# Two layers written out in one block of engine programs instead of a loop of blocks

## The chip, the core and the metric

One core of one Trainium2 chip. The metric is the device time of one execution in microseconds (us), the median of three. The engines are TensorE (PE; its weight loads are shown as PEld), VectorE (DVE), ScalarE (ACT), GpSimd (POOL) and SyncE (SP), which here issues the DMAs.

## What is computed

A token stream of 512 x 1024 floats passes through two layers (DEPTH = 2) and then a second block of another kind. All data are float32, and each layer is

```python
mod = c_act @ ada_w[l] + ada_b[l]
sh1, sc1, g1, sh2, sc2, g2, sh3, sc3, g3 = jnp.split(mod, N_MOD, axis=-1)
h = modulate(rms_norm(x, norm_ffn1[l]), sh1, sc1)
x = x + 0.5 * g1[:, None, :] * swiglu(h, ffn1_w_in[l], ffn1_w_out[l])
h = modulate(rms_norm(x, norm_mix[l]), sh2, sc2)
x = x + g2[:, None, :] * token_mix(h, cos, sin, mix_w_in[l], sgu_w[l], sgu_b[l], mix_w_out[l])
h = modulate(rms_norm(x, norm_ffn2[l]), sh3, sc3)
x = x + 0.5 * g3[:, None, :] * swiglu(h, ffn2_w_in[l], ffn2_w_out[l])
```

`swiglu` splits `h @ w_in` in two, takes `silu(a) * b` and multiplies by `w_out` (inner width 2816). `token_mix` joins a gated mixing of chunks of 128 tokens with an attention over the best 128 keys of each query. The second block (its own norms, a feed-forward, a recurrent and two attention branches, another feed-forward) follows the final norm; the change leaves its work alone.

## The kernel before

**Numbers.** A float32 product is made of three matmuls: every operand is held as a high part (`hH`, `guH`, `wH`) and a low part (`hL`, `guL`, `wL`), and `pe_3` (line 290) multiplies high by high (line 292), low by high or high by low (293, 294) into one PSUM bank, 128 x 512 outputs each.

**Weights.** They come in units of 128 x 2048 floats (1 MB; the output weights of a feed-forward have 3072 or 2560 a row), through a ring of two slots. For each unit SP issues the DMA into `wraw` once the low part of the unit two before it is done (`sp_units`, line 229, and `one` in `Ffn.sp`, line 576, issue at 234 and 578), ACT copies it rounded into `wH` (`act_high`, line 265), and POOL (`pool_low`, 242) or DVE (`dve_low`, 258) subtracts to get `wL`. PE waits for the low part. A unit of the input weights is 48 matmuls of line 292 to 294. The semaphores `full`, `high`, `low`, `mm` count units and tiles; `l_low` starts at 2, so "low >= u + 3" says that unit u is ready.

**A norm** (class `Norm`, 326) turns x into `hH` and `hL`. ACT squares the eight slices of x as they are updated (344), DVE adds six of them (353), PE sums over partitions (362, 367), DVE and ACT take the inverse root (377 to 387, 438 to 444), PE spreads it (393), and DVE scales (405), ACT adds the shift and rounds (432), DVE makes the low part (412). Between these PE runs matmuls on constants that nobody reads (`keep_warm`, 287). PE's first real matmul waits for slice 0 of `hL`.

**The modulation** (class `Modulation`, 638): the nine vectors of 1024 are products of silu(c) with rows of `ada_w`, made on DVE in the pauses of the feed-forwards (`mod_sum`, 669; each row tile is a DMA at 652), plus `mod_b` (663). The first two vectors of a layer are made by the layer before it, or, for layer 0, by the setup block.

**Blocks.** `nc.Block()` gives each engine one program; at its end all engines meet at a barrier. The kernel is: `setup_block`; then `with nc.Fori(0, layers) as l: layer_block(...)`, whose engine programs are compiled once and run twice, with l in a register; then `second_block`. At the end of each turn a further block of GpSimd alone clears the layer's 53 semaphores (`sem_clear`, 1695), so that each turn counts from zero. A turn begins with DMAs of its biases and gains (`mod_b` 1612, `gains` 1613), the copy of the first two modulation vectors (1662), the scale `m.A` (1602), and the first two units of weights, whose low parts are made by POOL (`pool_low`, called at 1631, timed at 247). The last feed-forward of a turn updates x in `dve_update` (620, timed at 626).

In a turn the order is norm 0, feed-forward 1, norm 1, mix, norm 2, feed-forward 2. At the two inner joints the first unit of the next stage is already asked for, rounded and split while the stage before it ends: `dve_update` is given `sizes=(..., self.ahead, 0)`, and ACT's matching step takes `self.ahead` (507). In feed-forward 2 `ahead` is 0.

The functions that the diff touches:

Of the kernel before, what the change touches and what calls it, by code (L numbers as in the profile page):

```python
# [58 lines left out]
L_FFN2 = L_MIX + MIX1_PROJ + 2 * OUT_UNITS  # L59
S_MEM = 0  # L60
# [29 lines left out]
def memory(nc):  # L90
# [103 lines left out]
    m.mod_b = small("mod_b", [N_MOD * KD])  # L194
# [3 lines left out]
    m.gains = small("gains", [3 * KD])  # L198
# [250 lines left out]
class Ffn:  # L449
# [85 lines left out]
    def dve(self, dve, nc, m, s, gate, mod=None, half_gate=None):  # L535
# [102 lines left out]
class Modulation:  # L638
# [6 lines left out]
    def __init__(self, w, in_a, in_b):  # L645
        self.w, self.in_a, self.in_b = w, in_a, in_b
# [778 lines left out]
def signals(nc, tag, first):  # L1425

    s = Signals()
    s.all = []

    def new(name):  # L1430
        s.all.append(nc.alloc_semaphore(f"{tag}_{name}"))
        return s.all[-1]
    s.full = [new("full0"), new("full1")]
    s.high = new("high")
    s.low = new("low")
    s.mm = new("mm")
    s.silu = new("silu")
    s.ufree = new("ufree")
    s.gu = new("gu")
    s.y = new("y")  # L1440
    s.sq = new("sq")
    s.acc = new("acc")
    s.ss = new("ss")
    s.var = new("var")
    s.rt = new("rt")
    s.dg = new("dg")
    s.spread = new("spread")
    s.tt = new("tt")
    s.hh = new("hh")
    s.hl = new("hl")  # L1450
# [58 lines left out]
def setup_block(nc, m, a):  # L1509
# [13 lines left out]
    with nc.Block() as block:  # L1523
        @block.sync
        def _(sp):
            sp.dma_start(m.pos[:], a["positions"].partition_broadcast(P)).then_inc(s.ld, 16)
            sp.dma_start(m.cst[:], a["constants"]).then_inc(s.ld, 16)
            sp.dma_start(m.c[:], a["c"].partition_broadcast(P)).then_inc(s.c, 16)
            sp.dma_start(m.x[:], a["x"]).then_inc(s.cx, 16)
            sp.dma_start(m.mod_b[:], a["ada_b"][LAYERS - 1]).then_inc(s.bias, 16)  # L1530

            for q in range(4):
                piece = a["ada_w"][LAYERS - 1, N_MOD - 2 + q // 2, 4 * (q % 2):4 * (q % 2) + 4]
                sp.dma_start(m.mod_big[:, q], piece.rearrange("t p k -> p t k")).then_inc(s.big[q], 16)

        @block.vector
        def _(dve):
# [24 lines left out]
            dve.wait_ge(s.bias, 16)  # L1562
            for c in range(2):
# [7 lines left out]
                nc.vector.tensor_tensor(m.mod[:, at + 2 * KD:at + 3 * KD], m.red[:], m.mod_b[:, at:at + KD], ALU.add)  # L1571
# [14 lines left out]
def layer_block(nc, m, s, a, l):  # L1586
    norms = [Norm(0, None, 0), Norm(1, 0, 1, y0=KD), Norm(2, 1, 2, y0=3 * KD),
             Norm(None, 2, None, y0=5 * KD)]
    ffn1 = Ffn(0, L_FFN1, 0, norms[0], norms[1], UNIT)
# [8 lines left out]
    def dve_scale_of(dve, n):

        dve.drain()  # L1600
        at = (3 * n + 1) * KD
        nc.vector.scalar_tensor_tensor(out=m.A[:], in0=m.mod[:, at:at + KD], scalar=1.0, in1=m.gains[:, n * KD:(n + 1) * KD],
                                       op0=ALU.add, op1=ALU.mult)
        dve.drain()

    with nc.Block() as block:
        @block.sync
        def _(sp):
            w_in = lambda g: (lambda i: a["ffn_in"][(2 * l + g) * IN_UNITS + i])
# [6 lines left out]
            sp.wait_ge(s.mod_used, 6 * KD + MOD_SLOTS)
            sp.dma_start(m.sguT[:], a["sgu_w"][l]).then_inc(s.par, 16)
            sp.dma_start(m.sgub[0:1], a["sgu_b"][l]).then_inc(s.par, 16)
            sp.dma_start(m.masks[:, 0:P], a["causal"]).then_inc(s.par, 16)
            for n, at in ((2, 2), (4, 8), (6, 6), (8, 4), (10, 10)):  # L1620
                sp_units(sp, m, s, lambda i: a["mix"][l, at + i], L_MIX + n, 2, UNIT)
            sp_mixed_out(sp, m, s, lambda i: a["mix"][l, MIX1_PROJ + i], L_MIX + MIX1_PROJ, 0)
            sp.wait_ge(s.ao, 4)
            sp.dma_start(m.c[:], a["c"].partition_broadcast(P)).then_inc(s.crow, 16)
            sp_mixed_out(sp, m, s, lambda i: a["mix"][l, MIX1_PROJ + i], L_MIX + MIX1_PROJ, 1)
            ffn2.sp(sp, m, s, w_in(1), w_a(1), w_b(1), mod2)

        @block.gpsimd
        def _(pool):
            pool.sem_inc(s.low, 2)  # L1630
            pool_low(pool, nc, m, s, L_FFN1, 2, UNIT)
            pool.wait_ge(s.low, L_MIX + 4)
            nc.gpsimd.memset(m.other[0][:], 0.0)
            nc.gpsimd.memset(m.other[1][:], 0.0).then_inc(s.clear, 1)
            pool_low(pool, nc, m, s, L_MIX + 2, 2, UNIT)

            pool.wait_ge(s.par, 80)
            nc.gpsimd.affine_select(out=m.sguT[:], in_=m.sguT[:], pattern=[[0, 4], [1, P]], compare_op=ALU.is_ge, fill=0.0,
                                    base=0, channel_multiplier=-1).then_inc(s.sgw, 1)
            mix.pool(pool, nc, m, s)  # L1640

        @block.scalar
        def _(act):
            act.sem_inc(s.silu, 2)
# [4 lines left out]
            ffn1.act(act, nc, m, s)
            norms[1].act_apply(act, nc, m, s, hH, shift(3))  # L1650
            mix.act(act, nc, m, s)
            norms[2].act_apply(act, nc, m, s, hH, shift(6))
            act.wait_ge(s.crow, 16)
            nc.scalar.activation(m.c[:], m.c[:], ACT.Silu).then_inc(s.csil, 1)
            ffn2.act(act, nc, m, s)

        @block.vector
        def _(dve):
            dve.sem_inc(s.ufree, 2)
            dve.sem_inc(s.y, 4)  # L1660
            dve.sem_inc(s.mod_used, MOD_SLOTS)
            nc.vector.tensor_copy(m.mod[:, 0:2 * KD], m.mod[:, N_MOD * KD:(N_MOD + 2) * KD])
            dve.wait_ge(s.par, 32)
            dve_scale_of(dve, 0)
            norms[0].dve_rsqrt(dve, nc, m, s)
# [302 lines left out]
```

## Time and profile before

| | |
|---|---|
| Median of three runs | 3103.42 us (3102.28 to 3119.74) |
| The profiled execution's own time | 3100.58 us |
| Its span, first to last instruction | 3098.9 us |
| Mean granted TensorE clock | 0.983 |
| PE busy | 2977.1 us, 96% of the span |
| DVE, ACT, POOL busy | 1567.0, 850.9, 284.9 us |

The span is made of the setup (0 to 37 us), layer 0 (to 1059), layer 1 (1067 to 2089) and the second block (2094 to 3098.9). Busy time of PE holds the matmuls of `keep_warm` too. A start-to-start distance of full-rate 128 x 512 matmuls is 0.23 us, though each is listed with 0.39 us, since they overlap.

### The profile page before, as it was taken

The page shows a single profiled execution, that of the slowest core. Times are in us where ns is not written, and L with a number is a line of the kernel's source. Part 1 is how long each engine was busy: PE and PEld are TensorE (multiplying, and loading weights), DVE is VectorE, ACT ScalarE, POOL GpSimd, SP SyncE. Part 2 cuts the span into 40 slices and gives each one's busy share as a digit, 9 for nine tenths or more (in the row PEclk, how much of TensorE's full clock was granted, in tenths as well). Part 3 has the DMA queues.
Part 4 walks back from the last instruction along what each step waited for, and adds up shares of the span by engine and source line. Part 5 has one row for each costly group of instructions (what it writes and reads, how often), then busy time and mean ns, then how long its engine had stood idle before and what let it go on. Part 6 is the DMA issues. An engine that isn't in the chain of part 4 may idle for free. (4 is left out here: it accounts for less than half of the span.)

```text
span 3098.9 us, 36454 instructions
## 1 busy us (share of the span) xinstructions
PE 2977.1 (96%) x13846; PEld 2444.8 (79%) x13846; DVE 1567.0 (51%) x2210; ACT 850.9 (27%) x957; POOL 284.9 (9%) x117
## 2 busy tenths in 40 slices
PE   4999999999999899999999999997999999999999
PEld 3888887778888688888877788875888878778887
DVE  6654647756524365365685653336332455553232
ACT  3222232332212232123323321214221235332121
POOL 1000015310000100000451000002000013100000
PEclk9999999999999899999999999997999999999999
DMA  5544522124523145353211453212322321133222
GB/s 216 205 162 149 190 89 89 42 75 162 190 81 105 64 171 191 117 188 120 88 57 36 159 194 109 98 51 104 108 108 82 107 76 48 35 109 107 83 98 78
DMA packets 61318, 351.88 MB, mean 114 GB/s; under 512 B 7698, under 2 KB 8082, under 8 KB 33556
## 3 DMA queue, kind: packets, MB, share of 16 engines
q1 hardware_dynamic: 60436, 348.99, 31.8%
q10 hardware_dynamic: 768, 1.44, 0.3%
q8 instruction: 63, 1.03, 0.1%
q14 instruction: 51, 0.42, 0.0%
HBM read 346.87 MB, written 2.10 MB: 113 GB/s over the span
## 5 line engine op out<-in xcount | busy, mean ns | idle before, releaser
L292 PE MATMUL bank<-m_hH,m_wH 128*128 128x512 f32 x2480 | 977.9, 394 | 21.1 <-DVE m_hL L412 17.3
L294 PE MATMUL bank<-m_hH,m_wL 128*128 128x512 f32 x2480 | 969.9, 391 | 0.0
L293 PE MATMUL bank<-m_hL,m_wH 128*128 128x512 f32 x2480 | 969.7, 391 | 0.0
L262 DVE TENSOR_TENSOR m_wL<-m_wraw,m_wH 128x2048 fp32r<-128x2048 f32 (+2 forms) x180 | 450.6, 2504 | 592.8 <-ACT m_wH L269 592.6
L269 ACT ACTIVATE m_wH<-m_wraw 128x2048 fp32r<-128x2048 f32 (+3 forms) x238 | 465.0, 1954 | 905.4 <-PE bank L294 900.6
L292 PEld LDWEIGHTS bank<-m_hH,m_wH 128*128 128x128 f32 x2480 | 467.7, 189 | 127.6 <-issue 26.4
L294 PEld LDWEIGHTS bank<-m_hH,m_wL 128*128 128x128 f32 x2480 | 467.6, 189 | 98.0
L293 PEld LDWEIGHTS bank<-m_hL,m_wH 128*128 128x128 f32 x2480 | 467.8, 189 | 94.4 <-issue 0.2
L292 PE MATMUL bank<-m_guH,m_wH 128*128 128x512 f32 (+1 forms) x1264 | 498.8, 395 | 1.5 <-DVE m_guL L846 1.5
L294 PE MATMUL bank<-m_guH,m_wL 128*128 128x512 f32 (+1 forms) x1264 | 491.5, 389 | 0.0
L293 PE MATMUL bank<-m_guL,m_wH 128*128 128x512 f32 (+1 forms) x1264 | 491.3, 389 | 0.0
L292 PEld LDWEIGHTS bank<-m_guH,m_wH 128*128 128x128 f32 x1264 | 237.9, 188 | 49.7 <-DVE m_guL L846 1.8
L294 PEld LDWEIGHTS bank<-m_guH,m_wL 128*128 128x128 f32 x1264 | 237.5, 188 | 49.0
L293 PEld LDWEIGHTS bank<-m_guL,m_wH 128*128 128x128 f32 x1264 | 237.9, 188 | 45.4
L247 POOL TENSOR_TENSOR m_wL<-m_wraw,m_wH 128x1024 fp32r<-128x1024 f32 (+1 forms) x42 | 141.8, 3381 | 1154.1 <-ACT m_wH L269 1154.1
L494 ACT ACTIVATE m_sg<-bank 128x512 f32<-128x512 f32 x132 | 78.7, 599 | 427.1 <-PE bank L294 426.8
L669 DVE CUSTOM_DVE_ANT_0 m_mod_w<-m_mod_w,m_c 128x1024 f32<-128x1024 f32 x144 | 171.1, 1224 | 26.0 <-DMA m_mod_w<-in_ada_w 12.8
L517 DVE TENSOR_TENSOR m_gut<-m_sg,bank 128x512 f32<-128x512 f32 x132 | 90.8, 688 | 157.2 <-PE bank L294 153.7
L626 DVE SCALAR_TENSOR_TENSOR m_x<-bank,m_gate,m_x 128x512 f32<-128x512 f32 x64 | 47.8, 750 | 208.5 <-PE bank L294 207.8
L344 ACT ACTIVATE m_sq<-m_x 128x512 f32<-128x512 f32 x70 | 44.0, 631 | 206.4 <-DVE m_x L626 204.4
L521 DVE TENSOR_TENSOR m_guL<-m_gut,m_guH 128x512 f32 (+1 forms) x132 | 91.4, 692 | 17.1 <-issue 0.8
L626 DVE SCALAR_TENSOR_TENSOR m_x<-bank,m_x 128x512 f32<-128x512 f32 x40 | 27.6, 691 | 140.5 <-PE bank L294 140.3
(234 smaller groups left out, 2259.9 us busy)
## 6 DMA issues: line engine op xcount, KB each, us to landing
m_wraw<-in_ffn_in SPq DMA_DIRECT2D x132, 1024.0 KB, 4.9
m_mod_w<-in_ada_w SPq DMA_DIRECT2D x144, 512.0 KB, 4.5
m_wraw<-in_ffn_out_a SPq DMA_DIRECT2D x24, 1536.0 KB, 7.7
m_wraw<-in_mix SPq DMA_DIRECT2D x32, 1024.0 KB, 4.9
m_wraw<-in_ffn_out_b SPq DMA_DIRECT2D x24, 1280.0 KB, 5.6
m_wraw<-in_mix SPq DMA_DIRECT2D x24, 512.0 KB, 3.8
m_mod_big<-in_ada_w SPq DMA_DIRECT2D x4, 2048.0 KB, 20.5
m_x<-in_x SPq DMA_DIRECT2D x1, 2048.0 KB, 9.3
```

Of the source, the lines that this page charges most:

```text
L247: nc.gpsimd.tensor_tensor(m.wL[:, j, 0:size], m.wraw[:, j, 0:size], f(m.wH[:, j, 0:size]), ALU.subtract)\
L262: nc.vector.tensor_tensor(m.wL[:, j, 0:size], m.wraw[:, j, 0:size], f(m.wH[:, j, 0:size]), ALU.subtract).then_inc(s.low, 1)
L269: nc.scalar.activation(m.wH[:, j, 0:size], m.wraw[:, j, 0:size], ACT.Copy).then_inc(s.high, 1)
L292: nc.tensor.matmul(out, a[0], b[0], start=first, stop=False)
L293: nc.tensor.matmul(out, a[0], b[1], start=False, stop=False)
L294: return nc.tensor.matmul(out, a[1], b[0], start=False, stop=last)
L344: nc.scalar.activation(out, x, ACT.Square).then_inc(s.sq, 1)
L494: nc.scalar.activation(m.sg[:, j], m.bank[j][:], ACT.Silu).then_inc(s.silu, 1)
L517: nc.vector.tensor_tensor(m.gut[:, j], m.sg[:, j], m.bank[2 + j][:], ALU.mult).then_inc(s.ufree, 1)
L521: nc.vector.tensor_tensor(m.guL[:, tile + j], m.gut[:, j], f(m.guH[:, tile + j]), ALU.subtract).then_inc(s.gu, 1)
L626: nc.vector.scalar_tensor_tensor(out=m.x[:, d], in0=m.bank[4 + d % 4][:], scalar=gate(d), in1=m.x[:, d], op0=ALU.mult, op1=ALU.add).then_i ...
L669: return nc.vector.tensor_tensor_reduce(out=w, in0=w, in1=m.c[:], scale=1.0, scalar=0.0, op0=ALU.mult, op1=ALU.add, accum_out=m.red[:, k:k ...
```

## The change

The loop and the clearing block go. `layers_block` makes two `Layer` objects and writes both layers' work one after the other into one program for each engine, in one `nc.Block()`. The 19 semaphores of the weight ring, the norms and the feed-forwards (`ring_signals`) are shared and counted through: unit, tile and norm numbers of layer 1 begin where layer 0 ends (`u = l * L_UNITS`, `y = l * 6 * KD`, `n = 3 * l`). The others exist once for each layer. The last feed-forward of layer 0 gets layer 1's first norm and `ahead = UNIT`, so layer 1's first unit is taken in as at the inner joints, and the second is split by DVE behind the norm; POOL does the first two units in layer 0 only. Biases and gains of both layers are loaded in the setup. A new hook `then` in `Ffn.dve` moves the making of `m.A` ahead of the last updates of x: for feed-forward 1, and across the layers also the copy of the two modulation vectors.

```diff
 def memory(nc):
-    m.mod_b = small("mod_b", [N_MOD * KD])
+    m.mod_b = small("mod_b", [LAYERS, N_MOD * KD])
-    m.gains = small("gains", [3 * KD])
+    m.gains = small("gains", [LAYERS, 3 * KD])
...
-    def dve(self, dve, nc, m, s, gate, mod=None, half_gate=None):
+    def dve(self, dve, nc, m, s, gate, mod=None, half_gate=None, then=None):
...
+        if then:
+            then()
         dve_update(dve, nc, m, s, self.uc, gate, self.after, sizes=(UNIT_B, UNIT_B, self.ahead, 0))
...
 def setup_block(nc, m, a):
-            sp.dma_start(m.mod_b[:], a["ada_b"][LAYERS - 1]).then_inc(s.bias, 16)
+            for l in range(LAYERS):
+                sp.dma_start(m.mod_b[:, l], a["ada_b"][l]).then_inc(s.bias, 16)
+                sp.dma_start(m.gains[:, l], a["gains"][l]).then_inc(s.bias, 16)
...
+class Layer:
+    def __init__(self, nc, m, s, a, l):
+        u, y, n = l * L_UNITS, l * 6 * KD, 3 * l
+        self.norms = [Norm(n, n - 1 if l else None, n, y0=y - KD), Norm(n + 1, n, n + 1, y0=y + KD),
+                      Norm(n + 2, n + 1, n + 2, y0=y + 3 * KD)]
...
+    def sp(self, sp, before):
+        if before:
+            sp.wait_ge(before.s.mod_used, N_MOD * KD + MOD_SLOTS)
+        self.ffn1.sp(sp, m, s, w_in(0), w_a(0), w_b(0), self.mod1)
...
+    def pool(self, pool):
+        if self.l == 0:
+            pool.sem_inc(s.low, 2)
+            pool_low(pool, nc, m, s, u + L_FFN1, 2, UNIT)
...
+    def act(self, act):
+        if self.l == 0:
+            act.sem_inc(s.silu, 2)
+            self.norms[0].act_sqrt(act, nc, m, s)
+            act_high(act, nc, m, s, 0, 0, 0, UNIT)
+            act_high(act, nc, m, s, 1, 1, 0, UNIT)
...
+    def dve_begin(self, dve):
+        dve.drain()
+        nc.vector.tensor_copy(m.mod[:, 0:2 * KD], m.mod[:, N_MOD * KD:(N_MOD + 2) * KD])
+        self.dve_scale_of(dve, 0)
+
+    def dve(self, dve, then):
+        dve.sem_inc(s.mod_used, MOD_SLOTS)
+        if self.l == 0:
+            self.dve_begin(dve)
+        self.norms[0].dve_rsqrt(dve, nc, m, s)
+        self.norms[0].dve_apply(dve, nc, m, s, hH, hL, scale, self.shift(0), u + L_FFN1 + 1 if self.l else None)
+        self.ffn1.dve(dve, nc, m, s, gate, self.mod1, half_gate=2, then=lambda: self.dve_scale_of(dve, 1))
...
+def layers_block(nc, m, a):
+    ring = ring_signals(nc, "l")
+    one, two = [Layer(nc, m, signals(nc, f"l{l}", True, ring), a, l) for l in range(LAYERS)]
+    one.follow(two.norms[0], UNIT)
+    two.follow(Norm(None, 5, None, y0=11 * KD), 0)
+    with nc.Block() as block:
+        @block.vector
+        def _(dve):
+            one.dve(dve, lambda: two.dve_begin(dve))
+            two.dve(dve, None)
...
-    with nc.Block() as block:
-        @block.gpsimd
-        def _(pool):
-            for x in s.all:
-                pool.sem_clear(x)
...
 def program(nc, a, layers=LAYERS, second=True, debug=None):
-    s = signals(nc, "l", True)
-    with nc.Fori(0, layers) as l:
-        layer_block(nc, m, s, a, l)
+    layers_block(nc, m, a)
```

Line numbers of the changed kernel differ from those of before: 626 becomes 629, 262 becomes 263, 353 354, 377 378, 405 406, 578 581, 652 655.

VectorE, end of a layer's feed-forward 2, before: the last tiles of x are updated (626), squares added (353), and the program ends in the loop's branch; `l_mm` counts finished tiles of PE.

```order
L262 TENSOR_TENSOR m_wL<-m_wraw,m_wH 128x2560 [waits l_high]
L353 TENSOR_TENSOR m_acc<-m_acc,m_sq 128x512 [waits l_sq]
L626 SCALAR_TENSOR_TENSOR m_x<-bank,m_gate,m_x 128x512 [waits l_mm]
L353 TENSOR_TENSOR m_acc<-m_acc,m_sq 128x512 [waits l_sq]
L626 SCALAR_TENSOR_TENSOR m_x<-bank,m_gate,m_x 128x512 [waits l_mm]
L353 TENSOR_TENSOR m_acc<-m_acc,m_sq 128x512 [waits l_sq]
L626 SCALAR_TENSOR_TENSOR m_x<-bank,m_gate,m_x 128x512 [waits l_mm]
L353 TENSOR_TENSOR m_acc<-m_acc,m_sq 128x512 [waits l_sq]
L626 SCALAR_TENSOR_TENSOR m_x<-bank,m_gate,m_x 128x512 [waits l_mm]
L1606 UNCONDITIONAL_BRANCH
L1832 REGISTER_ALU [waits barrier_Pool_Activation_PE_DVE_SP_release]
L1832 COMPARE_AND_BRANCH
```

The same place in the changed kernel, end of layer 0:

```order
L263 TENSOR_TENSOR m_wL<-m_wraw,m_wH 128x2560 [waits l_high]
L354 TENSOR_TENSOR m_acc<-m_acc,m_sq 128x512 [waits l_sq]
L629 SCALAR_TENSOR_TENSOR m_x<-bank,m_gate,m_x 128x512 [waits l_mm]
L354 TENSOR_TENSOR m_acc<-m_acc,m_sq 128x512 [waits l_sq]
L629 SCALAR_TENSOR_TENSOR m_x<-bank,m_gate,m_x 128x512 [waits l_mm]
L263 TENSOR_TENSOR m_wL<-m_wraw,m_wH 128x2048 [waits l_high,l_low]
L354 TENSOR_TENSOR m_acc<-m_acc,m_sq 128x512 [waits l_sq]
L629 SCALAR_TENSOR_TENSOR m_x<-bank,m_gate,m_x 128x512 [waits l_mm]
L354 TENSOR_TENSOR m_acc<-m_acc,m_sq 128x512 [waits l_sq]
L629 SCALAR_TENSOR_TENSOR m_x<-bank,m_gate,m_x 128x512 [waits l_mm]
L378 TENSOR_SCALAR m_nt<-bank 128x4 [waits l_ss]
```

The split of layer 1's first unit (the 128x2048 row) now stands among the updates, and the norm follows the last update with no branch or barrier between.

SyncE, begin of the layer, before: bias and gains stand ahead of the first weights.

```order
L1613 ISA
L1613 DMA m_gains<-in_gains 128x24
L578 ISA [waits l_low]
L578 DMA m_wraw<-in_ffn_in 128x2048
L578 ISA [waits l_low]
L578 DMA m_wraw<-in_ffn_in 128x2048
L584 UNCONDITIONAL_BRANCH
```

SyncE, from the setup into layer 0, in the changed kernel (`m_mod_big` is what the setup needs of `ada_w`):

```order
L1542 DMA m_mod_b<-in_ada_b 128x72
L1543 DMA m_gains<-in_gains 128x24
L1542 DMA m_mod_b<-in_ada_b 128x72
L1543 DMA m_gains<-in_gains 128x24
L1547 DMA m_mod_big<-in_ada_w 128x4x1024 x4
L1534 UNCONDITIONAL_BRANCH
L1733 UNCONDITIONAL_BRANCH [waits barrier_Pool_Activation_PE_DVE_SP_release]
L581 DMA m_wraw<-in_ffn_in 128x2048 [waits l_low] x2
```

The four small DMAs (one stood there before) are now ahead of `m_mod_big`, and the first thing behind the barrier is the weights.

## Rows read from the trace of the kernel before

**Rows 1.** Page: busy us of each engine, share of the span, instructions.

```profile
PE 2977.1 (96%) x13846; PEld 2444.8 (79%) x13846; DVE 1567.0 (51%) x2210; ACT 850.9 (27%) x957; POOL 284.9 (9%) x117
```

**Rows 2.** Timeline of PE from layer 0 into layer 1 (start, us, what, idle before).

```profile
1067.78 1.84 PE L362 MATMUL bank<-m_ones,m_acc 128*128 128x1 f32 x8 [9.98 <-issue]
...
1080.16 0.47 PE L292 MATMUL bank<-m_hH,m_wH 128*128 128x512 f32 x1 [2.71 <-DVE m_hL L412]
...
1085.02 0.80 PE L292 MATMUL bank<-m_hH,m_wH 128*128 128x512 f32 x1 [2.42 <-DVE m_hL L412]
```

**Rows 3.** Timelines of ACT, DVE, POOL and SP over the same joint.

```profile
1058.62 0.63 ACT L344 ACTIVATE m_sq<-m_x 128x512 f32<-128x512 f32 x1 [6.16 <-DVE m_x L626]
...
1080.60 4.37 DVE L412 SCALAR_TENSOR_TENSOR m_hL<-m_t,m_mod,m_hH 128x512 fp32r<-128x512 f32 x1
...
1074.92 9.49 POOL L247 TENSOR_TENSOR m_wL<-m_wraw,m_wH 128x2048 fp32r<-128x2048 f32 x2 [395.54 <-ACT m_wH L269]
...
1066.89 0.34 SPq L1612 DMA_DIRECT2D m_mod_b<-in_ada_b  x1
```

**Rows 4.** Queue instructions of the clearing and the loop: min/median/max ns, first and last start.

```profile
L1695 POOLq EVENT_SEMAPHORE_RANGE_CLEAR  x106: 44/44/48, 1059.5 to 2093.1; - x106
...
L1832 ACTq COMPARE_BRANCH  x2: 40/42/45, 1063.6 to 2093.5; - x2
...
L1832 PEldq COMPARE_BRANCH  x2: 76/1988/3900, 1063.7 to 2093.6; - x2
```

**Rows 5.** Timeline of PE at layer 0's joint from feed-forward 1 into the mix.

```profile
415.81 0.95 PE L362 MATMUL bank<-m_ones,m_acc 128*128 128x1 f32 x8
417.48 1.05 PE L367 MATMUL bank<-m_ones,m_sq 128*128 128x1 f32 x8 [0.72 <-ACT m_sq L344]
...
424.97 0.47 PE L292 MATMUL bank<-m_hH,m_wH 128*128 128x512 f32 x1 [1.55 <-DVE m_hL L412]
```

**Rows 6.** Windows: us, busy (instructions) of PE, PEld, DVE, ACT, POOL, PEclk, DMA share, GB/s.

```profile
10.00:30.00 20.00, 0.00 (x0) 0.00 (x0) 16.73 (x29) 5.95 (x10) 0.00 (x0) 1.00 1.02 408
...
415.58:424.97 9.39, 7.13 (x36) 5.95 (x35) 4.21 (x12) 5.29 (x6) 0.00 (x0) 0.82 0.00 0
...
685.00:698.36 13.36, 8.65 (x36) 7.19 (x35) 6.77 (x16) 5.93 (x7) 0.00 (x0) 0.74 0.42 157
...
698.36:720.36 22.00, 22.00 (x97) 18.04 (x97) 17.22 (x22) 9.70 (x11) 0.00 (x0) 1.00 0.17 51
1057.41:1080.16 22.75, 10.07 (x36) 8.29 (x35) 5.70 (x13) 7.16 (x7) 5.24 (x2) 0.62 0.27 98
1080.16:1108.31 28.15, 25.73 (x96) 20.46 (x97) 18.50 (x20) 8.51 (x10) 4.25 (x1) 0.82 0.29 112
1085.02:1090.00 4.98, 4.98 (x12) 3.92 (x13) 4.98 (x8) 2.55 (x4) 0.00 (x0) 0.50 0.80 322
...
1445.52:1454.58 9.06, 7.14 (x37) 6.01 (x35) 4.22 (x12) 5.30 (x6) 0.00 (x0) 0.81 0.00 0
```

**Rows 7.** Timelines of ACT, PE and SP from layer 1 into the second block.

```profile
2088.54 0.63 ACT L344 ACTIVATE m_sq<-m_x 128x512 f32<-128x512 f32 x1 [6.17 <-DVE m_x L626]
...
2093.86 1.84 PE L362 MATMUL bank<-m_ones,m_acc 128*128 128x1 f32 x8 [6.14 <-PEq L1691]
```

**Rows 8.** Timelines from the setup into layer 0, engine by engine.

```profile
37.56 1.84 PE L362 MATMUL bank<-m_ones,m_acc 128*128 128x1 f32 x8 [37.56 <-PEq L1523]
...
32.11 1.22 DVE L669 CUSTOM_DVE_ANT_0 m_mod_big<-m_mod_big,m_c 128x1024 f32<-128x1024 f32 x1 [0.16 <-DMA m_mod_big<-in_ada_w]
...
36.86 0.17 DVE L1571 TENSOR_TENSOR m_mod<-m_red,m_mod_b 128x8 f32<-128x8 f32 x1
...
44.15 1.91 ACT L269 ACTIVATE m_wH<-m_wraw 128x2048 fp32r<-128x2048 f32 x1 [2.60 <-DMA m_wraw<-in_ffn_in]
...
37.55 0.37 SPq L1612 DMA_DIRECT2D m_mod_b<-in_ada_b  x1
...
38.68 12.57 SPq L578 DMA_DIRECT2D m_wraw<-in_ffn_in  x3
```

More of the change, by code:

```diff
@@ L1420, in act_mixed_out, with ring_signals, signals @@
         act_squares(act, nc, m, s, after, q, u + q, HALF if q < OUT_UNITS - 2 else UNIT)
-def signals(nc, tag, first):
-    s = Signals()
[L1428 to L1450, printed above, removed]
+def ring_signals(nc, tag):
+    r = Signals()
+    new = lambda name: nc.alloc_semaphore(f"{tag}_{name}")
+    r.full = [new("full0"), new("full1")]
+    r.high = new("high")
+    r.low = new("low")
+    r.mm = new("mm")
+    r.silu = new("silu")
+    r.ufree = new("ufree")
+    r.gu = new("gu")
+    r.y = new("y")
+    r.sq = new("sq")
+    r.acc = new("acc")
+    r.ss = new("ss")
+    r.var = new("var")
+    r.rt = new("rt")
+    r.dg = new("dg")
+    r.spread = new("spread")
+    r.tt = new("tt")
+    r.hh = new("hh")
+    r.hl = new("hl")
+    return r
+def signals(nc, tag, first, r):
+    s = Signals()
+    new = lambda name: nc.alloc_semaphore(f"{tag}_{name}")
+    s.full, s.high, s.low, s.mm = r.full, r.high, r.low, r.mm
+    s.silu, s.ufree, s.gu, s.y = r.silu, r.ufree, r.gu, r.y
+    s.sq, s.acc, s.ss, s.var, s.rt, s.dg, s.spread = r.sq, r.acc, r.ss, r.var, r.rt, r.dg, r.spread
+    s.tt, s.hh, s.hl = r.tt, r.hh, r.hl
     s.ev = new("ev")
@@ L1561, in _ @@
             dve.wait_ge(s.sil, 1)
-            dve.wait_ge(s.bias, 16)
+            dve.wait_ge(s.bias, 16 * 2 * LAYERS)
             for c in range(2):
@@ new lines, in pe @@
+    def pe(self, pe):
+        nc, m, s = self.nc, self.m, self.s
+        if self.l == 0:
+            pe.sem_inc(s.mm, 4)
+        self.norms[0].pe_sum(pe, nc, m, s)
+        self.norms[0].pe_spread(pe, nc, m, s)
+        self.ffn1.pe(pe, nc, m, s)
+        self.norms[1].pe_sum(pe, nc, m, s)
+        self.norms[1].pe_spread(pe, nc, m, s)
+        self.mix.pe(pe, nc, m, s)
+        self.norms[2].pe_sum(pe, nc, m, s)
+        self.norms[2].pe_spread(pe, nc, m, s)
+        self.ffn2.pe(pe, nc, m, s)
@@ L1616, in _ @@
[L1616 to L1626, printed above, removed]
+            one.sp(sp, None)
+            two.sp(sp, one)
         @block.gpsimd
         def _(pool):
-            pool.sem_inc(s.low, 2)
-            pool_low(pool, nc, m, s, L_FFN1, 2, UNIT)
-            pool.wait_ge(s.low, L_MIX + 4)
@@ L1633, in _ @@
[L1633 to L1640, printed above, removed]
+            one.pool(pool)
+            two.pool(pool)
@@ L1654, in _ @@
-            nc.scalar.activation(m.c[:], m.c[:], ACT.Silu).then_inc(s.csil, 1)
-            ffn2.act(act, nc, m, s)
+            one.act(act)
+            two.act(act)
         @block.vector
         def _(dve):
[L1659 to L1665, printed above, removed]
@@ L1687, in _ @@
-            norms[2].pe_sum(pe, nc, m, s)
-            norms[2].pe_spread(pe, nc, m, s)
-            ffn2.pe(pe, nc, m, s)
-    with nc.Block() as block:
-        @block.gpsimd
-        def _(pool):
-            for x in s.all:
-                pool.sem_clear(x)
+            one.pe(pe)
+            two.pe(pe)
 def second_block(nc, m, s, a):
```

127 lines of the change are left out of this document (73 added, 54 removed).

## The prediction

> **What bounds the kernel now.** I read the page's busy times first: PE is busy 2977.1 of 3098.9 us, every other engine 51% or less [rows 1]. So only two things can change the time: fewer or faster matmuls, which the change does not touch, or less time in which PE does nothing useful. The change acts at joints, so I went on to the timelines there, and then to windows that begin and end at a matmul, which give the length of a stretch of equal work.
>
> Four joints lie between the parts: setup to layer 0, layer 0 to layer 1, layer 1 to the second block, and within the layers the joints that already run without a barrier. The last kind is my yardstick. At the joint from feed-forward 1 into the mix the first real matmul starts 9.39 us after the start of the last one before it in layer 0, 9.06 us in layer 1 [rows 6]. From layer 0 to layer 1 the same distance is 22.75 us [rows 6]. The reader is to see in it that PE could not even begin the norm's sums before 1067.78 (idle 9.98 us, ended by nothing but "issue") [rows 2], while at the inner joint the sums begin at 415.81, 0.23 us after the last matmul's start at 415.58 [rows 5, 6].
>
> **Layer 0 to layer 1, before.** ACT's last square ends at 1058.62 + 0.63 = 1059.25 [rows 3]. Then the barrier, 53 clears on POOL (106 in both turns, the first at 1059.5) and a second barrier, after which every engine branches at 1063.6 [rows 4]. Behind the branch the engines come back 3 us later: SP's first DMA is at 1066.89 [rows 3], and PE's own branch takes up to 3.90 us, which is the longer of its two [rows 4]. That longer one I take for the taken jump back, the 76 ns one for the exit. So of the 7.6 us from 1059.25 to 1066.89 some 4.3 us are barriers and clears and 3.3 us the jump.
>
> The Trainium skill has this jump in "Runtime: NRT & Kernel Launch", section Instruction fetch mechanics: "Branching breaks sequential prefetch", a taken branch out of the window of held pages waits for a fetch. By that rule the loop costs its jump once for each backward turn, as the row shows, and writing out is the cure; the same rule could charge a jump at the new exit, which is a rival below.
>
> **What replaces it.** After the change there is nothing between the last update and the norm; unit 0 of layer 1 is split on DVE among the updates and unit 1 behind the norm, as at the inner joints. SP's new wait on `mod_used` of layer 0 asks for row tiles that DVE consumes beside the first input weights of feed-forward 2, long before its last output weights, so it holds nothing; SP's waits on layer 1's own `mod_used` open when DVE enters layer 1, just after the last update, and behind them stands only the DMA of unit 3, which has unit 1's split to wait for anyway. I take the yardstick's 9.39 for the new distance:
> 22.75 - 9.39 = **13.4 us gained** (bounds: a distance of 9.06, or the 13.36 of the joint from mix to feed-forward 2 [rows 6], which would give 9.4).
>
> **The first two units behind the joint.** From its first matmul to the 97th (two units of 48) layer 1's feed-forward 1 takes 28.15 us; feed-forward 2 of layer 0, the same work with the split on DVE, takes 22.00 [rows 6]. Two causes, both seen: POOL splits two units from 1074.92 for 9.49 us, and beside it a DVE low part lasts 4.37 us [rows 3], so that PE waits until 1085.02, 4.86 us after its first matmul [rows 2], where six matmuls take 1.4 (22.00 / 97 = 0.227 each); and then TensorE has the granted clock 0.50 between 1085 and 1090, its lower level of 1.2 GHz, after 22.75 us in which it was granted 0.62 [rows 6]. After the shorter joint of the yardstick the granted clock was 0.82 within and 1.00 in the units that follow [rows 6]. With POOL out and the gap short, both go:
> 28.15 - 22.00 = **6.15 us gained** (bounds 3.5, which is 4.86 - 1.4, if only the waiting goes and the clock does not come back, and 6.5).
>
> **Layer 1 to the second block.** ACT ends at 2088.54 + 0.63 = 2089.17, PE starts the next sums at 2093.86 [rows 7]: 4.69 us with one block's barrier, 53 clears, a second barrier and the loop's exit. After the change one barrier is left. What one barrier costs is seen behind the setup: DVE ends at 36.86 + 0.17 = 37.03 and PE starts at 37.56, 0.53 us later [rows 8]. 4.69 - 0.53 = **4.1 us gained**. The second block's start hangs on its own DMAs as well, but these are issued behind the same barrier, so all of it moves together. Bounds: 0.8, if the exit pays the 3.3 us of the jump, and 4.2.
>
> **Setup to layer 0.** SP issued the bias from 37.55 and reached the weights at 38.68 [rows 8]: 1.13 us, now gone from there. ACT had waited 2.60 us for those weights until 44.15 [rows 8], more than 1.13, and the first matmuls hang on ACT's and POOL's work behind them: **1.1 us gained**. Against it, three more small DMAs stand ahead of `m_mod_big`. DVE is already waiting for the last piece of that (0.16 us at 32.11) [rows 8], and the DMA engines are full before it: share 1.02, 408 GB/s [rows 6]; so any delay lands on DVE and on the end of the setup. Lower bound: 60 KB (36, 12 and 12) at 408 GB/s is 0.15 us. Upper bound: three issues of 0.57 us, as the two from 37.55 to 38.68 took [rows 8], 1.7 us. I take **0.4 us lost**, nearer the first, since SP's issues run ahead of the queue.
>
> **Edits costed at nothing.** Making `m.A` ahead of the updates of feed-forward 1: before, it lies where DVE waits for PE's sums, which wait for ACT's last square (PE idle 0.72 before its second sums) [rows 5]; an instruction of that size takes 0.17 us [rows 8], so with its drains some 0.3 us at each of two joints would come back or be lost if that reading were wrong. Offsets that are constants rather than registers save work on SP, whose queue is ahead all the time: nothing. The longer tables move addresses only.
>
> **Sum.** -13.4 - 6.15 - 4.1 - 1.1 + 0.4 = **-24.4 us**. Against the profiled execution's own 3100.58 us that is 3076.2. The median of the runs shown is 2.8 us above it and the lowest run 1.7 above; 3103.4 - 24.4 = 3079.0 and 3102.3 - 24.4 = 3077.9. I take 3078.
>
> **Rivals.**
> (a) *The joint does not close as the inner one does* (the change does less than it says). Feed-forward 2 ends with the same updates as feed-forward 1, but another wait, such as unit 0's split late on DVE, could give the 13.4 us distance of the other inner joint. Then 4.0 us less: 3082. For it: DVE also has the splits of 2560-wide units there. Against it: it has them at the yardstick too, in the same order.
> (b) *The exit pays a jump.* 3.3 us less, 3081. For it: 3.3 us behind the backward branch. Against it: the forward branches behind the setup took 0.53 us with the barrier. Here the Trainium skill's rule of the page named above speaks for the loss only if the target lies outside what is held; in program order it lies next.
> (c) *Much more than the sum, faster by over 1%.* It takes 31 us, so 6.6 beyond the sum. PE is idle 3098.9 - 2977.1 = 121.8 us in all [rows 1], of which 37.6, 10.0 and 6.1 stand at the three barriers [rows 8, 2, 7]. Only if the written-out layers also ran their 40 inner backward turns (below) tighter, by 0.2 us each, would it come there: 3070.
> (d) *Slower.* The loops inside the feed-forwards stay loops, on PE two of five turns and two of two in each, so 10 backward jumps, 40 in the four feed-forwards of the layers. The program is now longer and each loop lies at other addresses. If the body of a loop no longer lay wholly in what the engine holds, each backward turn would cost what PE's jump cost, 3.90 us [rows 4]. Seven such jumps (7 x 3.9 = 27.3) use up the gain; the four of one loop in each of the four feed-forwards would be 16 x 3.9 = 62 us, so 3078 + 62 = 3140. For it: the price is in the trace. Against it: feed-forward 2 did two units in 22.00 us, which is 97 starts of 0.227, so in this kernel no inner turn pays it, at several addresses.
>
> **How the numbers follow.** Forecast 0.70; (a) 0.10; (b) 0.07; (c) 0.08; (d) 0.05. A difference of 1% (31 us) is about what a measurement of this kernel can tell from no change. The forecast, (a) and (b) lie within it: 0.87; faster by over 1% is (c), 0.08; slower is (d), 0.05. The range: the gains' lower bounds together (9.4 + 3.5 + 0.8 + 1.1 - 1.7 = 13.1) would give 3090, but not all at once; the upper (13.7 + 6.5 + 4.2 + 1.1 - 0.15 = 25.4) gives 3077 from the median and 3075 from the profiled time. With some of (c) below and (a) and (b) above: 3071 to 3086.
>
> **What would show each step.** The distance from the last matmul of layer 0 to the first of layer 1 should be 9 to 10 us, with sums of PE starting within 0.5 us; the following 96 matmuls in 22 us at clock 1.00, no DVE low part over 1 us there, and no POOL split; no clears; PE's sums of the second block about 0.5 us behind ACT's last square; first weights of layer 0 asked for as the first thing behind the setup, and `m_mod_big` late by less than 1 us. A joint of over 13 us would make (a) right, a PE start 3 to 4 us behind ACT's last square (b), and inner loops with gaps of 3 us on PE (d).

## The result and the profile after

| | median | lowest to highest | runs |
|---|---|---|---|
| before, in the same session | 3118.14 us | 3101.74 to 3130.42 | 13 |
| changed | 3080.47 us | 3074.68 to 3102.62 | 13 |

The ratio is 0.9909, interval 0.9881 to 0.9937: faster by 0.9%. It compares the means, 3114.6 and 3086.2 us; the medians of the table are 37.7 us apart. The interval excludes no change and holds 1%. The time lies in the range (3071 to 3086), 2.5 us above the forecast. Both kernels' runs fall into groups. Before: five runs at 3101.7 to 3103.5, six at 3117.9 to 3120.8, two at 3130. Changed: seven at 3074.7 to 3080.5, three at 3088.1 to 3089.9, three at 3101.7 to 3102.6. Between the medians of the lowest groups, 3103.4 and 3078.1, lie 25.3 us, where the sum said 24.4. The groups were not in the prediction; what they are is the larger part of what follows.

The profiled execution of the changed kernel, at 3101.67 us, is of its uppermost group. From the page, PE's busy time and its granted clock in 40 slices:

```profile
PE 2996.5 (97%) x13846; PEld 2457.0 (79%) x13846; DVE 1567.5 (51%) x2212; ACT 851.5 (27%) x957; POOL 275.2 (9%) x115
...
PEclk9999999799999999999988999997999999999999
```

As many matmuls as in [rows 1], yet PE is busy for 19.4 us longer: something lengthened them, in the slices with 7 and 8. The same line before has an 8 in the 14th slice and the 7 in the 28th, but neither the 7 in the 8th nor the two 8s in the 21st and 22nd:

```profile
PEclk9999999999999899999999999997999999999999
```

First the joints. Timeline of PE from layer 0 into layer 1 (as [rows 2]):

```profile
1070.25 0.39 PE L295 MATMUL bank<-m_guH,m_wL 128*128 128x512 f32 x1
1070.48 0.95 PE L363 MATMUL bank<-m_ones,m_acc 128*128 128x1 f32 x8
1072.14 1.05 PE L368 MATMUL bank<-m_ones,m_sq 128*128 128x1 f32 x8 [0.72 <-ACT m_sq L345]
...
1078.25 0.47 PE L293 MATMUL bank<-m_hH,m_wH 128*128 128x512 f32 x1 [1.55 <-DVE m_hL L413]
```

The sums start 0.23 us behind the last matmul, not 10 us, and the rest reads as [rows 5] do. Windows of the joint and of the 97 matmuls behind it (as [rows 6]: us, busy of PE, PEld, DVE, ACT, POOL, then the clock):

```profile
1070.25:1078.25 8.00, 5.74 (x36) 4.58 (x35) 4.05 (x11) 5.30 (x6) 0.00 (x0) 1.00 0.36 131
1078.25:1100.24 21.99, 21.99 (x96) 18.02 (x97) 17.09 (x21) 8.53 (x10) 0.00 (x0) 1.00 0.14 49
```

POOL is idle in both. DVE's timeline has the split of layer 1's first unit among the updates, and low parts of 0.75 us where 4.37 stood [rows 3]:

```profile
1060.40 2.29 DVE L263 TENSOR_TENSOR m_wL<-m_wraw,m_wH 128x2048 fp32r<-128x2048 f32 x1 [2.57 <-ACT m_wH L270]
...
1077.35 0.75 DVE L413 SCALAR_TENSOR_TENSOR m_hL<-m_t,m_mod,m_hH 128x512 fp32r<-128x512 f32 x1
```

Timelines of the engines at the exit into the second block (as [rows 7]) and, below, from the setup into layer 0 (as [rows 8]):

```profile
2095.20 0.63 ACT L345 ACTIVATE m_sq<-m_x 128x512 f32<-128x512 f32 x1 [6.16 <-DVE m_x L629]
...
2096.29 1.02 PE L363 MATMUL bank<-m_ones,m_acc 128*128 128x1 f32 x8 [1.91 <-PEq L1732]
```

```profile
37.25 0.17 DVE L1584 TENSOR_TENSOR m_mod<-m_red,m_mod_b 128x8 f32<-128x8 f32 x1
37.68 11.73 SPq L581 DMA_DIRECT2D m_wraw<-in_ffn_in  x3
...
42.35 1.91 ACT L270 ACTIVATE m_wH<-m_wraw 128x2048 fp32r<-128x2048 f32 x1 [0.50 <-DMA m_wraw<-in_ffn_in]
...
49.58 0.47 PE L293 MATMUL bank<-m_hH,m_wH 128*128 128x512 f32 x1 [2.06 <-DVE m_hL L413]
```

The exit takes 2096.29 - 2095.83 = 0.46 us (before 4.69). The setup ends at 37.42 (37.03), the weights are asked for at 37.68 (38.68) and reach ACT 1.80 us earlier.

**Where the 19 us went.** PE's pause before the attention of layer 0, in the kernel before and then in the changed one; the score matmul waits for DVE, then a projection does:

```profile
586.32 0.32 PE L292 MATMUL bank<-m_kH,m_qH 64*128 64x128 f32 x1 [1.24 <-DVE m_ra L1098]
...
587.60 0.51 PE L292 MATMUL bank<-m_guH,m_wH 128*128 128x512 f32 x1 [0.74 <-DVE m_guL L846]
```

```profile
584.20 0.32 PE L293 MATMUL bank<-m_kH,m_qH 64*128 64x128 f32 x1 [1.23 <-DVE m_ra L1102]
...
585.48 0.49 PE L293 MATMUL bank<-m_guH,m_wH 128*128 128x512 f32 x1 [0.74 <-DVE m_guL L850]
```

The same pauses to 0.01 us. Windows behind them, before and then changed (layer 0, layer 1):

```profile
587.00:621.00 34.00, 33.40 (x190) 24.77 (x190) 17.86 (x67) 13.51 (x42) 4.75 (x2) 1.00 0.16 54
```

```profile
587.00:621.00 34.00, 34.00 (x110) 24.76 (x108) 9.83 (x39) 8.96 (x27) 4.72 (x2) 0.50 0.15 47
...
1611.00:1645.10 34.10, 34.10 (x111) 25.08 (x111) 9.90 (x40) 8.95 (x27) 4.72 (x2) 0.51 0.13 47
```

In this execution the granted clock is at its lower level, 1.2 GHz, for 34 us at the attention of each layer: 110 matmuls where the kernel before did 190. Each costs 14.6 to 14.7 us (layer 0 from first to last matmul 1020.67 against 1006.05 us), 29.3 together, and hides the whole gain in this one execution: span 3099.9 against 3098.9.

### The profile page after: what moved, and what is told of

Same layout as the page of the kernel before. It is cut to its first block and busy times, and to the rows that moved or that the text cites. A ratio compares the mean times of both kernels' runs of the same rounds, so it can differ in the third digit from the quotient of the medians.

```text
span 3099.9 us, 35954 instructions
## 1 busy us (share of the span) xinstructions
PE 2996.5 (97%) x13846; PEld 2457.0 (79%) x13846; DVE 1567.5 (51%) x2212; ACT 851.5 (27%) x957; POOL 275.2 (9%) x115
## 5 line engine op out<-in xcount | busy, mean ns | idle before, releaser
L248 POOL TENSOR_TENSOR m_wL<-m_wraw,m_wH 128x1024 fp32r<-128x1024 f32 (+1 forms) x40 | 132.2, 3309 | 785.2 <-ACT m_wH L270 785.2
## 6 DMA issues: line engine op xcount, KB each, us to landing
m_mod_big<-in_ada_w SPq DMA_DIRECT2D x4, 2048.0 KB, 17.7
```

What stands on the lines that cost most here:

```text
L248: nc.gpsimd.tensor_tensor(m.wL[:, j, 0:size], m.wraw[:, j, 0:size], f(m.wH[:, j, 0:size]), ALU.subtract)\
```

## The experiments

Ten runs, three of them of the two kernels unchanged. "Sum" below is the distance of the joint plus the 97 matmuls behind it: 22.75 + 28.15 = 50.90 us before [rows 6], 8.00 + 21.99 = 29.99 changed.

### e1: the kernel before, its loop written out

```diff
-    with nc.Fori(0, layers) as l:
+    for l in range(layers):
```

> The kernel before with its layer loop written out in the program: both turns keep their own block, the clearing block and the barriers; only the jump back is gone. Measured by the stretch from the last matmul of layer 0 to the 97th of layer 1 (before 22.75 + 28.15 = 50.9 us, changed kernel 8.00 + 21.99 = 30.0). Theory (the loop's taken jump costs 3.3 us): 47.6 us, +-0.5. Rival (any entry into a new block costs as much as the jump back): 50.9 us.

Measured: one run, 3126.2 us, with both of the long falls of the clock. ACT's last square and PE's sums on the timeline, then the windows of joint and 97 matmuls:

```profile
1072.26 0.63 ACT L344 ACTIVATE m_sq<-m_x 128x512 f32<-128x512 f32 x1 [6.17 <-DVE m_x L626]
...
1077.35 1.84 PE L362 MATMUL bank<-m_ones,m_acc 128*128 128x1 f32 x8 [5.92 <-PEq L1691]
```

```profile
1071.04:1090.01 18.97, 9.86 (x36) 8.29 (x35) 5.66 (x13) 7.16 (x7) 5.24 (x2) 0.73 0.31 114
1090.01:1115.42 25.41, 23.45 (x96) 18.77 (x97) 18.48 (x20) 8.52 (x10) 4.26 (x1) 0.94 0.32 124
```

Sum 44.38, where 47.6 was expected: a miss. 3.8 us are off the distance and 2.7 off the stretch behind it. But that second part is not the jump's: two more profiles of the kernel before (e6, e9), which have the jump, also take 25.42 there, at granted clocks of 0.94 and 0.93 (0.82 before, 0.94 here), with distances of 23.69 and 23.54, so sums of 49.0 to 50.9. Against e6 and e9 the loop costs 4.6 to 4.7 us. The jump is read best without the clock, from the end of ACT's last square to PE's sums: 1067.78 - 1059.25 = 8.53 us before [rows 2, 3], here 1077.35 - 1072.89 = 4.46. It is 8.56 in e6 and 8.43 in e9. The jump costs PE 4.07 us, near its own branch of 3.90 [rows 4] rather than the 3.3 that I took from SP.

### e2: the changed kernel with one border between the layers

No loop and no clears; each layer in a block of its own, layer 1's first two units rounded and split by POOL behind the border.

```diff
-    one.follow(two.norms[0], UNIT)
-    with nc.Block() as block:
...
+    one.follow(Norm(None, 2, None, y0=5 * KD), 0)
+    for layer in (one, two):
+        with nc.Block() as block:
...
-        if self.l == 0:
-            pool_low(pool, nc, m, s, u + L_FFN1, 2, UNIT)
+        pool_low(pool, nc, m, s, u + L_FFN1, 2, UNIT)
```

> The changed kernel with a block border (one barrier) between the layers again, no loop, no clears, and layer 1's first two units taken in behind the border and split by POOL, as before. Theory (jump 3.3, clears and second barrier 4.0, bias and gain DMAs ahead of the weights 1.1 to 2.2): 50.9 - 8.4 to 9.5 = 41.4 to 42.5 us for the same stretch. Rival (the barrier itself is the price, clears and jump are hidden behind something else): over 47 us.

Measured: 3090.28 us, sum 41.63, as expected. The windows, then ACT's last square and PE's sums:

```profile
1057.87:1072.01 14.14, 8.82 (x36) 7.34 (x35) 5.34 (x11) 7.16 (x7) 5.24 (x2) 0.73 0.37 149
1072.01:1099.50 27.49, 25.53 (x96) 20.36 (x97) 18.41 (x20) 8.51 (x10) 4.25 (x1) 0.83 0.30 115
```

```profile
1059.08 0.63 ACT L345 ACTIVATE m_sq<-m_x 128x512 f32<-128x512 f32 x1 [6.17 <-DVE m_x L629]
1060.02 1.06 PE L363 MATMUL bank<-m_ones,m_acc 128*128 128x1 f32 x8 [1.76 <-PEq L1733]
```

ACT's last square ends at 1059.71, so the border itself takes 0.31 us, and the clears and the other barrier were 4.46 - 0.31 = 4.15 us. The bias DMAs, for which 1.1 to 2.2 us were expected, stand behind PE's sums, not in this difference; no run shows their part alone. Yet the border costs more than its 0.31. PE's first sums need only seven of eight slices; without a border they run beside the last square, 0.23 us behind the last matmul, with one 2.15 us behind it.

### e3: no border, but POOL splits the first two units

```diff
-    one.follow(two.norms[0], UNIT)
+    one.follow(two.norms[0], 0)
...
-        if self.l == 0:
-            pool_low(pool, nc, m, s, u + L_FFN1, 2, UNIT)
+        pool_low(pool, nc, m, s, u + L_FFN1, 2, UNIT)
```

> The changed kernel with no border, but layer 1's first two units are again rounded by ACT behind the inverse root and split by POOL. Theory (the early take-in and the split on DVE are a gain of their own): the stretch is 36 to 38 us, 6 to 8 more than the changed kernel's 30.0, with DVE low parts of over 4 us beside POOL. Rival (once the barrier is gone the two units are ready in time): 30 to 31 us.

Measured: 3096.96 us (one of the two long falls), sum 37.24, as expected. Windows, then DVE's timeline:

```profile
1069.17:1079.67 10.50, 5.73 (x37) 4.59 (x35) 6.01 (x11) 6.94 (x7) 5.24 (x2) 1.00 0.00 0
1079.67:1106.41 26.74, 23.94 (x97) 19.21 (x97) 18.40 (x20) 8.52 (x10) 4.25 (x1) 0.87 0.31 119
```

```profile
1076.80 2.72 DVE L413 SCALAR_TENSOR_TENSOR m_hL<-m_t,m_mod,m_hH 128x512 fp32r<-128x512 f32 x1 [0.67 <-ACT m_hH L433]
...
1080.10 4.36 DVE L413 SCALAR_TENSOR_TENSOR m_hL<-m_t,m_mod,m_hH 128x512 fp32r<-128x512 f32 x1
```

Long low parts are back as soon as POOL subtracts beside them, at full clock in the joint too. Behind the joint the stretch is 4.75 us longer (26.74 - 21.99): PE is idle for 2.80 of them, and 1.95 are matmuls at a lower granted clock (0.87). In the joint it is 2.5 us: 1.97 are the low part of 2.72 us (0.75 elsewhere); the rest is ACT, which rounds the second unit ahead of its first `hH`. The Trainium skill, "SBUF — State Buffer", section SBUF: two separate sides, says that a VectorE operation with two SBUF inputs and a GpSimd one that reads SBUF take a shared port in turns, for a whole instruction each; the trace agrees, 4.36 us where 0.75 is the usual and one POOL subtraction takes 4.74.

### e4 and e5: TensorE kept at work before the attention

Eight matmuls on constants before the wait for the attention's operands, four before the first projection, put into the changed kernel (e4) and into the one before (e5). Nobody reads them.

```diff
+        pe.wait_ge(s.ev, 22)
+        keep_warm(nc, m, 0, 8)
         pe.wait_ge(s.ao, 4)
-        self.attention.pe(pe, nc, m, s)
+        self.attention.pe(pe, nc, m, s, 4)
...
+                if g == 0:
+                    keep_warm(nc, m, 0, warm)
```

> The changed kernel with 8 idle matmuls ahead of PE's wait before the attention and 4 more ahead of its first output tile, in both layers. Theory (the granted clock falls where PE pauses before the attention and then stays at 0.50 for tens of us in some runs): no stretch at 0.50 between the mix projections and feed-forward 2 except behind norm 2, mean clock 0.987 or more, all runs within 5 us of the fastest, 3073 to 3079 us; the idle matmuls themselves cost under 1 us a layer. Rival (the falls come by chance inside the attention, whatever precedes it): the same spread as the changed kernel, 3075 to 3102 us, with about half of the runs over 3085.

> The kernel before with the same idle matmuls ahead of the attention in both turns of its loop. Theory (the upper group of the kernel before, 3115 to 3130 us, are runs in which the clock falls at the attention): every run at 3100 to 3103 us, none over 3110. Rival (the groups of the kernel before come from elsewhere, the joints or the second block): about half of the runs over 3115 still.

Measured: e4 3074.66 us (six runs, 3073.37 to 3079.47), ratio 0.9893 (0.9868 to 0.9917). e5 3103.7 us (ten runs, 3099.42 to 3108.63), ratio 0.9963 (0.9928 to 0.9999); beside it six of 13 runs of the kernel before lay at 3114 to 3134, and the other seven at 3098.8 to 3103.0, with a median of 3101.4. Neither has an upper group left. The lower one did not stay as expected: six of e5's ten runs lie over 3103, its median 2.3 us above that of the seven, and one run of e4 is 6.1 us above its fastest. Timeline of PE in e4, and its windows:

```profile
583.49 2.01 PE L288 MATMUL bank<-m_warm 128*128 128x512 f32 x8
585.90 1.19 PE L288 MATMUL bank<-m_warm 128*128 128x512 f32 x4
```

```profile
583.00:592.00 9.00, 9.00 (x46) 6.72 (x45) 4.22 (x13) 3.03 (x8) 1.15 (x1) 1.00 0.18 58
592.00:632.00 40.00, 40.00 (x236) 29.69 (x235) 21.48 (x73) 15.94 (x46) 5.97 (x3) 1.00 0.16 53
```

With the pauses of 1.24 and 0.74 us filled the long falls are gone, in 16 of 16 runs; with them open the clock falls in some executions and not in others, in both kernels (e9 has a fall in the kernel before), so the change did not bring it. Which of the two pauses matters was not tried, nor whether a wait of the same length without matmuls would do as little harm.

### e6, e9, e10: the two kernels profiled again, unchanged

> The kernel before, unchanged, for another profile. If its time is over 3110 us, theory: a stretch of some 34 us at granted clock 0.50 from about 588 or 1618 us, and each such stretch explains 13 to 15 us; rival: the clock is the same as in the first profile there and the time lies elsewhere. If it is near 3102, no such stretch in either layer.

> The kernel before once more, for a profile of its upper group (3114 to 3134 us in 4 to 6 of 13 runs). Theory: over 3110 us only with stretches of granted clock 0.50 of over 10 us from about 588 or 1618 us on, at 13 to 15 us for each of 34; near 3102 with at most 3.4 us there. Rival: a time over 3110 without them.

> The changed kernel once more, for a profile of its lower group. Theory: 3075 to 3080 us with at most 3.4 us at 0.50 at the attention of either layer, the joint and the exit as in its first profile (8.0 to 9.4 and 0.5 us); or over 3088 with one long stretch, over 3100 with two. Rival: the groups differ elsewhere.

Measured: e6 3102.81 us, of the lowest group, no long fall. e9 3117.6 us, of the middle one. Windows of e9 (the attention of layer 0, the joint, the attention of layer 1), and the last of the kernel before:

```profile
592.00:632.00 40.00, 40.00 (x238) 30.21 (x239) 22.40 (x76) 16.57 (x49) 7.11 (x3) 1.00 0.17 51
...
1058.10:1081.64 23.54, 8.58 (x36) 7.17 (x35) 5.70 (x13) 7.17 (x7) 5.21 (x2) 0.71 0.26 95
1081.64:1107.06 25.42, 23.46 (x96) 18.78 (x97) 18.49 (x20) 8.52 (x10) 4.25 (x1) 0.93 0.33 124
...
1618.00:1652.00 34.00, 34.00 (x111) 25.08 (x111) 9.97 (x40) 8.95 (x27) 4.72 (x2) 0.51 0.14 47
```

```profile
1618.00:1652.00 34.00, 34.00 (x194) 25.08 (x192) 17.31 (x64) 13.50 (x41) 4.75 (x2) 1.00 0.15 47
```

One long fall, in layer 1, and a span 14.8 us above e6's: the middle group of the kernel before has one long fall. The changed kernel's middle group lies 10 us above its lowest, not 14.6, and was not profiled. e10, the changed kernel at 3080.13 us, has no long fall. But behind the same pause in layer 0 its matmuls are at the lower level for some 3 us (granted clock 0.96 from 587 to 621), as in e6 in both layers (0.95), while the first profile of before has 1.00: the clock falls there for 34 us, for a few, or not at all. The joint of e10:

```profile
1057.98:1067.37 9.39, 7.12 (x37) 5.95 (x35) 4.05 (x11) 5.30 (x6) 0.00 (x0) 0.82 0.33 112
1067.37:1089.36 21.99, 21.99 (x96) 18.02 (x97) 17.09 (x21) 8.52 (x10) 0.00 (x0) 1.00 0.14 49
```

### e7 and e8: can the start and the joints give more?

e7 is e4 with the first two units of weights asked for in the setup (whose `m_mod_big` moves to other memory for them), ACT's rounding of them ahead of the inverse root, and the second unit split by DVE instead of POOL. e8 is e7 with more idle matmuls in the norms of both blocks.

```diff
+            for j in range(2):
+                sp.dma_start(m.wraw[:, j, 0:UNIT], a["ffn_in"][j]).then_inc(ring.full[j], 16)
...
-            self.norms[0].act_sqrt(act, nc, m, s)
             act_high(act, nc, m, s, 0, 0, 0, UNIT)
             act_high(act, nc, m, s, 1, 1, 0, UNIT)
+            self.norms[0].act_sqrt(act, nc, m, s)
```

```diff
-        self.norms = [Norm(n, n - 1 if l else None, n, y0=y - KD), ...
+        self.norms = [Norm(n, n - 1 if l else None, n, y0=y - KD, warm=(0, 6, 8)), ...
```

> The changed kernel with the idle matmuls of e4, and with the first two units of weights of layer 0 loaded already in the setup (the setup's tile of modulation weights moved to other memory so that both fit), rounded by ACT ahead of its inverse root, unit 1 split by DVE behind the norm. Theory (layer 0's start hangs on weights and on POOL beside DVE, as layer 1's did): first matmul at about 48.4 us rather than 49.6, the seventh 2.6 us behind it at the lower clock level rather than 4.8, no DVE low part over 2 us, 3 to 5 us off e4: 3070 to 3072 us. Rival (the weights' 2 MB delay the setup's last modulation weights by as much): no gain, 3074 to 3076.

> e7 with more idle matmuls at the norms of the layers and of the second block's two last norms: 8 instead of 4 ahead of the first real matmul, and 10 where PE waits 3.2 us for the last square sums at the joint from mix to feed-forward 2. Theory (what is left of half clock behind each norm, 3.4 to 10 us at a time, comes from those pauses): 1.7 us for each 3.4 us of half clock taken away at six joints, up to 10 us off e7. Rival (idle matmuls behind the norm delay the real ones): each costs 0.22 us where the pause is shorter, so 0 to 3 us slower than e7.

Measured: e7 3069.38 us (four runs, 3068.35 to 3073.78), ratio 0.9856 (0.9786 to 0.9926). The first matmul came at 50.03, not 48.4: a miss; the time is a little under the 3070 to 3072 expected. Timelines of ACT, DVE and PE in e7:

```profile
38.38 3.71 ACT L270 ACTIVATE m_wH<-m_wraw 128x2048 fp32r<-128x2048 f32 x2 [20.96 <-PEq L1725]
...
42.11 1.28 ACT L388 ACT_TABLE_LOAD   x1
43.40 0.20 ACT L388 ACTIVATE m_nr<-m_nv 128x4 f32<-128x4 f32 x1
...
43.90 1.05 DVE L441 SCALAR_TENSOR_TENSOR m_nt<-m_nr 128x4 f32<-128x4 f32 x1
...
50.03 0.76 PE L293 MATMUL bank<-m_hH,m_wH 128*128 128x512 f32 x1 [0.77 <-DVE m_hL L413]
```

ACT's two roundings and the table load behind them put the root at 43.40, on the path of the norm. What came as expected lies behind: six matmuls on at 2.69 us (4.85 in the changed kernel), the 97th at 23.55 where e4 has 28.13. e8: 3067.64 us (four runs, 3066.82 to 3069.52), ratio 0.9852 (0.9782 to 0.9922), 1.7 us under e7 and within the spread of both, where up to 10 were expected: a miss. Windows of its joint between the layers:

```profile
1049.63:1059.03 9.40, 8.05 (x41) 6.74 (x39) 4.04 (x11) 5.29 (x6) 0.00 (x0) 0.82 0.32 112
1059.03:1080.80 21.77, 21.77 (x96) 17.85 (x97) 16.89 (x21) 8.52 (x10) 0.00 (x0) 1.00 0.14 49
```

PE is busy for 8.05 of 9.40 us instead of 7.12 of 9.39, and the clock is 0.82 as before. The added matmuls come too late to hold it: the six ahead of them already take 2.55 us on e8's timeline, 1.65 in the profile after, whose clock stays at 1.00. e7 and e8 are both faster than the kernel before, and their eight runs (up to 3073.78) lie below the fastest of the changed kernel (3074.68), though these were taken in another session. The gain of e7 over e4 is across sessions too.

## Where the prediction was right, and which step failed

**The step that failed** is the one from the sum to the chances, "lie within it: 0.87", which took a gain under 1% for no change. It has two parts. The sum gave nothing to TensorE's granted clock at the attention, without a reason: there a long fall costs 14.6 to 14.8 us in some executions and nothing in others, and it put 15 us between the median of the three runs shown (3103.4) and that of 13 (3118.1). And the prediction took 1% (31 us) as what a measurement of this kernel can hardly tell from no change, which no row shows. The measured interval, 0.9881 to 0.9937, excludes no change: 0.9% was a clear gain. The lowest groups alone are 25.3 us apart, and the lowest group of before spans 1.8 us, that of the changed kernel 5.8, so the 24.4 of the sum, 0.79%, can be told from nothing.

Terms of the sum, from the spans of two profiles of the changed kernel against the one of before:

| | predicted | profile after | e10 |
|---|---|---|---|
| setup to the first matmul | -0.7 | -1.78 | -1.56 |
| layer 0, first to last matmul | 0 | +14.62 | +2.13 |
| joint and 97 matmuls | -19.55 | -20.91 | -19.52 |
| layer 1 from there to its last square | 0 | +14.73 | +0.02 |
| exit to the second block's sums | -4.1 | -4.23 | -4.23 |
| second block | 0 | -1.43 | +2.66 |
| sum | -24.4 | +1.0 | -20.5 |

**The joint** was right in mechanism and size. In e10 it is 9.39 + 21.99 us, the yardstick's 9.39 and feed-forward 2's 22.00 to the hundredth; in the profile after the distance is 1.4 us shorter, since the clock stayed at 1.00 in it, 0.82 in e10. Rival (a), 13.4 us, fell.

**What the 22.75 us were** was right in kind: a jump, and barriers with clears. The jump's size was off, 4.07 us on PE (e1) where I wrote 3.3, read from SP's first DMA. The Trainium skill, "Runtime: NRT & Kernel Launch", section Instruction fetch mechanics, gives no price for a taken branch; this one is e1's.

**The 97 matmuls.** Both causes hold, POOL's subtraction (e3) and the clock. But 28.15 was one draw: the same kernel took 25.42 in e6 and e9, with a longer joint. The pair is steadier (49.0 to 50.9) than its halves, and from e6 and e9 to e10 the gain is 17.6 to 17.7, not 19.5.

**The exit**: 0.46 us, no jump paid forward; rival (b) fell.

**The start**: the setup's delay of 0.39 us was the 0.4 predicted, but that is one pair of profiles: e10 against e6 it is 0.14. The other half, 1.1 us from the bias DMAs, was mis-sized: the weights reached ACT 1.80 us earlier. Why 0.8 more than the issue moved stays open.

**(c) and (d)**: layer 1 behind its 97th matmul took 980.88 us in e10 and 980.86 before. The inner loops run neither tighter nor with jumps. What 2.13 us in layer 0 and 2.66 in the second block of e10 are stays open; both have no term.

**What had no term** was the granted clock at the attention. I read the profile of before as the kernel, but it was one of three kinds of execution: none, one or two long falls. That 3080.5 lies so near the forecast of 3078 is in part luck: the profile that I worked from had no long fall, and seven of 13 runs of the changed kernel had none either, just enough to put its median there. The spread of the three runs, 3102.28 to 3119.74, showed a second group, and I passed it over. Rival (c) was the only way past 1% that I named, and its mechanism did not happen; the missing one was this. That the changed kernel has fewer long falls than the one before is not shown: by their times six of its 13 runs have one or two, eight of 13 before.

**In the range** the upper sum of gains, 25.4, leads from the median to 3078, not 3077; nothing hangs on it.

## What to carry to other kernels

Write out a loop whose turn is one long stage, and cost the joint by an inner joint of the same kernel that already runs free: here that gave the distance exactly in one of two profiles (9.39 us, the other 8.00). Of the 19.0 to 20.9 us gained on the sum, 4.4 came with the border (41.63 in e2, 37.24 in e3) and 7.25 with the early take-in and the split on DVE (37.24, 29.99): most came from what may now overlap, not from the jump. When a few runs of a kernel differ by more than 0.3%, find the stretch that makes the groups before any sum is set against their median; here twelve idle matmuls at one place took the upper groups away in 16 runs of two kernels. In the lower group they gave nothing that is shown: the changed kernel was 3.4 us faster with them (in another session), the one before 2.3 us slower.

## What the hardware showed that I had not expected

TensorE's granted clock can sit at 0.50 for 34 us while PE is listed busy for all of it (34.00 of 34.00 us, 110 matmuls), after pauses of 1.24 and 0.74 us that in another execution of the same kernel leave it at 1.00. The Trainium skill, "TensorE: Matmul & The Clock Gate", section A second HAM failure mode: psum-queue depth-cycling, tells of frequent short idles between groups of matmuls, in another kernel, with which the clock goes up and down between its two levels. The traces fit it in part: filling the two pauses took the long falls away in 16 of 16 runs, but here one place in a layer goes before the fall, and with the same pauses some executions have none. What decides it in one execution stays open. A border of one barrier between two blocks took PE 0.31 to 0.53 us where nothing jumps back, and the sums that it kept from starting early some 1.9 more (2.15 us behind the last matmul instead of 0.23, e2); a jump back costs 4.07 us on PE.
